# Twenty-four conv and pool pairs and the loop over token chunks: where the side work stands among them

## The reference, cut to what matters

```python
x = layer_norm(x, ln0_g, ln0_b)                  # (2048, 1024)
h = x @ w_in                                     # conv value | conv gate | pool input | queries
a = a_val * sigmoid(a_gate)                      # 384 channels
a = silu(layer_norm(depthwise_conv31(a) + b))
p = trailing_means(p_in, windows 2,4,8,16) - p_in  # 4 groups of 96 channels
p = (p @ pool_w per group) * scale
k, v = mem @ w_mk, mem @ w_mv                    # 256 memory tokens, 4 heads
o = softmax(q @ k.T / 8) @ v
x1 = layer_norm(ALPHA * x + concat(a, p, o) @ w_out)
u = causal_depthwise_conv3(x1 @ w_up)            # 2 x 2816 channels
out = layer_norm(ALPHA * x1 + (silu(u_g) * u_v) @ w_down)
```

## Time and profile before

| what | value |
|---|---|
| median of 3 runs | 2013.52 us (2012.64 to 2013.69) |
| the profiled execution's own time | 2015.45 us |
| its span | 2013.7 us |
| PE busy over the span | 1890.2 us (94%) |
| DVE / ACT / POOL busy | 1483.1 / 940.1 / 259.9 us |
| mean granted clock of PE | 0.976 |

### The profile page before, as it was taken

How to read it: one execution, slowest core, us unless ns; L and a number is a source line. 1 busy time by engine, 2 the same in 40 slices (tenths; PEclk the granted TensorE clock), 3 DMA queues, 4 the chain that set the end, 5 groups by cost and what they waited for, 6 DMA issues and landing times.

```text
span 2013.7 us, 26244 instructions
## 1 busy us (share of the span) xinstructions
PE 1890.2 (94%) x8722; PEld 1572.2 (78%) x8722; DVE 1483.1 (74%) x1892; ACT 940.1 (47%) x1598; POOL 259.9 (13%) x339
## 2 busy tenths in 40 slices
PE   6999998769999899999999899999999897999997
PEld 5788888658788678888888688888887686887786
DVE  5534226558989788888887888778777767566898
ACT  2211124545555465655656665555556334224321
POOL 1101022102212412122120011000000000000111
PEclk9999998979999999999999899999999998999999
DMA  6422234444443834334345333212214557547543
GB/s 219 167 100 84 68 103 145 138 147 146 157 141 136 283 126 146 137 133 143 132 142 188 126 117 134 84 73 94 83 73 162 202 201 281 183 162 262 184 156 126
DMA packets 171788, 296.14 MB, mean 147 GB/s; under 512 B 11713, under 2 KB 106177, under 8 KB 171713
## 3 DMA queue, kind: packets, MB, share of 16 engines
q1 hardware_dynamic: 171712, 295.18, 42.4%
HBM read 189.23 MB, written 105.91 MB: 147 GB/s over the span
## 4 chain that ended last, share of the span: by engine, by line
PE 64%; DVE 11%; DMA 4%; ACT 3%; issue 3%; POOL 0%; SPq 0%; DVEq 0%; ACTq 0%; POOLq 0%
PE banks L2145 54%; PE banks L1090 4%; PE banks L1108 2%; DVE mov_lo L2342 2%; DMA y_scratch<-up_and_out 1%; DMA mov_raw<-wdown_sums_scratch 1%; PE banks L1023 1%; PE banks L1072 1%; DVE sta_lo L2338 1%; DMA mov_raw<-x_operands 1%; ACT mov_hi L2214 1%; PE banks L1054 1%; DVE up_and_out L2376 1%; DVE probs L1542 1%; PE banks L1153 0%
## 5 line engine op out<-in xcount | busy, mean ns | idle before, releaser
L2145 PE MATMUL banks<-mov_hi,sta_hi 128*128 128x512 f32 x1848 | 726.2, 393 | 40.1 <-ACT banks L2221 21.1
L2145 PE MATMUL banks<-mov_lo,sta_hi 128*128 128x512 f32 x1848 | 723.5, 392 | 0.0
L2145 PE MATMUL banks<-mov_hi,sta_lo 128*128 128x512 f32 x1848 | 723.5, 391 | 0.0
L2145 PEld LDWEIGHTS banks<-mov_hi,sta_hi 128*128 128x128 f32 x1848 | 350.2, 190 | 119.4 <-ACT banks L2221 22.7
L2145 PEld LDWEIGHTS banks<-mov_hi,sta_lo 128*128 128x128 f32 x1848 | 349.5, 189 | 73.9
L2145 PEld LDWEIGHTS banks<-mov_lo,sta_hi 128*128 128x128 f32 x1848 | 350.2, 190 | 72.2
L2338 DVE TENSOR_TENSOR sta_lo<-sta_raw,sta_hi 128x512 fp32r<-128x512 f32 (+1 forms) x340 | 224.0, 674 | 62.7 <-ACT sta_hi L2207 60.7
L2207 ACT ACTIVATE sta_hi<-sta_raw 128x512 fp32r<-128x512 f32 (+1 forms) x340 | 198.6, 611 | 135.4 <-PE banks L2145 103.2
L275 PE MATMUL banks<-x0t_hi,win_hi 128*128 128x512 f32 x320 | 126.5, 395 | 1.6 <-DVE x0t_lo L397 1.6
L2236 ACT ACTIVATE half_sums<-banks 128x512 f32<-128x512 f32 x68 | 40.7, 599 | 183.8 <-PE banks L2145 183.8
L275 PE MATMUL banks<-x0t_hi,win_lo 128*128 128x512 f32 x320 | 124.8, 390 | 0.0
(11 more groups left out here) (227 smaller groups left out, 2829.3 us busy)
## 6 DMA issues: line engine op xcount, KB each, us to landing
sta_raw<-in_w_up SPq DMA_DIRECT2D x88, 512.0 KB, 4.1
hidden_scratch<-up_and_out SPq DMA_DIRECT2D x44, 512.0 KB, 2.6
y_scratch<-up_and_out SPq DMA_DIRECT2D x16, 1024.0 KB, 7.5
sta_raw<-hidden_scratch SPq DMA_DIRECT2D x32, 512.0 KB, 4.4
up_and_out<-y_scratch SPq DMA_DIRECT2D x16, 1024.0 KB, 4.9
x_operands<-x_operands_out SPq DMA_DIRECT2D x56, 256.0 KB, 4.1
mov_raw<-x_operands SPq DMA_DIRECT2D x14, 1024.0 KB, 7.3
mov_raw<-in_w_down SPq DMA_DIRECT2D x44, 256.0 KB, 4.6
```

The lines of the kernel that those rows point to most:

```text
L2145: last = pe.matmul(psum, w, x, start=(start and k == 0 and i == 0), stop=(stop and k == m - 1 and i == 2), skip_group_check=True)
```

## The change

- **Start of the pairs.** The last two stores of queries leave the first block's SP list and open the second's; their wait moves to m = 1. PE's wait for the identity moves from before pair 0 to m = 13.
- **Keys, values, fold.** On PE keys go from m = 3 to 4, values from 6 to 7, fold(1) from 11 to 10, scores(0, 1) from 10 to 11; ACT and DVE parts move by a step with them. `bands_out` goes from 5 to 8.
- **Pool pairs in their own places.** Their high and low parts get six buffers of their own (`gp_h`, `gp_l`) instead of those in w_out's last rows; the pool bands move too. So `wout_hi(n >= 3)` waits for the 24 conv groups alone.
- **w_out's last rows** (n = 3 to 7) are loaded and split at m = 15, 16, 18, 20, 21 instead of behind the pairs; conv_total(1, 1) and squares(1, 1), mean(1), deviations(1, 1) come earlier or later as the orders below show. The first two quarters of `project(0)` become `project_first`, which takes the pool rows last.
- **Chunk loop.** `turned_lo(c, 1)` and `turned_hi(c, 1)` come before affine and residual 2 (DVE) and before norm, swish and pooled_hi (ACT); `operand_sums` of all chunks but the last go from POOL to DVE, before `normalise(c, 1)`.

```diff
+            if not is_conv(m):
+                act.wait_ge(prep_lo, 4)
+            act.activation(halves(m)[0][:, :, LEAD:LEAD + QS], gx_raw[:, m % 4, :, :], ACT.Copy).then_inc(gx_hi, 1)
...
-            sp.wait_ge(q_stored, 16 * QT * SEQ // 512)
+            store_last_queries(sp)
...
+                if m in (17, 18, 20):
+                    load_wo({17: 5, 18: 6, 20: 7}[m])
             store_pair(NP - 1)
-            load_wo(5)
-            load_wo(6)
...
-            rstds(0, None)
-            with pool.Fori(1, NCH) as c:
-                rstds(c, c - 1)
-            operand_sums(NCH - 1)
+            with pool.Fori(0, NCH) as c:
+                rstds(c)
+            last_operand_sums()
...
+            def project_first():
+                tok, pooled = slice(0, P), range(CT, 2 * CT)
+                pe.wait_ge(o_lo, 1)
+                pe.wait_ge(c_lo, 1)
+                for ks in ([k for k in range(KT) if k not in pooled], pooled):
+                    if ks is pooled:
+                        pe.wait_ge(p_l, 1)
+                    for b in range(2):
...
-            pe.wait_ge(ident_ok, 3)
             for m in range(NP):
                 pair(m)
-                if m == 3:
+                if m == 4:
                     keys()
-                if m == 6:
+                if m == 7:
                     values()
...
                 if m == 10:
+                    fold(1)
+                if m == 11:
                     scores(0, 1)
-                if m == 11:
-                    fold(1)
                 if m == 13:
+                    pe.wait_ge(ident_ok, 3)
...
                 if m == 21:
+                    turn(1, 1)
                     variance(0)
-                    turn(1, 1)
                 if m == 23:
                     pe.wait_ge(o_lo, 1)
                     attend(1)
+                    pe.wait_ge(c_std, 1)
+                    mean(1)
...
-                    act.wait_ge(g_mm, NG)
+                    act.wait_ge(g_mm, CONV_GROUPS)
...
+                if before2 is not None:
+                    dve.wait_ge(x1t_out, 4 * (before2 + 1))
+                    operand_sums(dve, before2)
                 normalise(c, 1)
...
                 turned_lo(c, 0)
                 scale_conv(c, s)
+                turned_lo(c, 1)
                 if before is not None:
                     affine(before, 0)
                     residual(before, 2)
-                turned_lo(c, 1)
                 conv_lo(c, s)
```

More of the change, by code:

```diff
@@ L139, in columns, with store_queries @@
             return slice(sum(COLS[:part]), sum(COLS[:part + 1]))
+        def store_queries(sp, c):
+            for t in range(QT):
+                row = D_CONV + D_POOL + t * P
+                dst = mix_d[row:row + P, :].rearrange("p (r h q) -> p r h q", r=PHASES, h=2)[:, 4 * (c % 2):4 * (c % 2) + 4, c // 2, :]
+                sp.dma_start(dst, qb[:, t, :].rearrange("p (u q) -> p u q", u=TT)).then_inc(q_stored, 16)
         def turns_behind(c, n):
@@ L678, in groups_done, with halves @@
             return 2 * ORDER.index(n // 2) + n % 2 + 1
+        def halves(m):
+            if is_conv(m):
+                return gx_h[:, m % 3, :, :], gx_l[:, m % 3, :, :]
+            return gp_h[m % 3], gp_l[m % 3]
         def band_place(n):
@@ L714, in store_last_operands, with operand_sums @@
                 sp.dma_start(xop_d[row:row + P, :], src.rearrange("p k t -> p (k t)")).then_inc(done, 16)
+        def operand_sums(eng, c):
+            low_a, up_a, low_b, up_b = xt[:, 0, 0:4, :], xt[:, 0, 4:8, :], xt[:, 1, 0:4, :], xt[:, 1, 4:8, :]
+            if not (isinstance(c, int) and c == 0):
+                eng.wait_ge(xop_stored, 16 * 7 * c)
+            eng.tensor_tensor(xs[:, 0, :, :], up_b, low_b, ALU.subtract).then_inc(x1_sums, 1)
+            eng.tensor_tensor(xs[:, 1, :, :], low_b, low_a, ALU.subtract).then_inc(x1_sums, 1)
+            eng.wait_ge(x1_sums, 4 * c + 2)
+            eng.tensor_tensor(xs[:, 2, :, :], up_b, xs[:, 1, :, :], ALU.subtract).then_inc(x1_sums, 1)
+            eng.wait_ge(x1_sums, 4 * c + 3)
+            eng.tensor_tensor(xs[:, 3, :, :], up_a, xs[:, 2, :, :], ALU.subtract).then_inc(x1_sums, 1)
         def load_x0(sp, c, u):
@@ L982, in _ @@
             last.then_inc(counts_ok, 1)
-            pool.wait_ge(prep_hi, 1)
+            pool.wait_ge(prep_hi, 2)
             for s in used:
@@ L1091, in project @@
                 last.then_inc(y_ready, 1)
+            def project_first():
[6 more added lines that the diff above has]
+                    for b in range(2):
+                        cols = slice(b * 512, (b + 1) * 512)
+                        for k in ks:
+                            for i, (w, x) in enumerate(exact_parts(mx_hi[0][:, k, tok], mx_lo[0][:, k, tok], wo_hi[:, k, cols], wo_lo[:, k, cols])):
+                                last = pe.matmul(ps_y[:, b, :], w, x, start=(k == 0 and i == 0), stop=(k == 2 * CT - 1 and i == 2))
+                        if ks is pooled:
+                            last.then_inc(y_ready, 1)
             def pair(m):
@@ L1098, in pair @@
                     pe.wait_ge(g_out, 2 * m - 4)
[L1099 removed]
+                h, l = halves(m)
                 if is_conv(m):
@@ L1216, in chunk @@
                     turn_x1(before, 0)
-            mean(1)
             pe.wait_ge(wo_l, KT)
-            project(0, 0, 0)
-            project(0, 0, 1)
+            project_first()
             variance(1)
@@ L1396, in _ @@
                     turned_hi(0, 0)
+                if m == 15:
+                    wout_hi(3)
                 if m == 16:
                     turned_hi(0, 1)
+                    wout_hi(4)
                 if m == 17:
@@ L1402, in _ @@
                     attn_hi(0, 0)
+                    wout_hi(5)
                 if m == 19:
@@ L1407, in _ @@
                     turned_hi(1, 0)
+                    wout_hi(6)
+                if m == 21:
+                    wout_hi(7)
                 if m == 22:
@@ L1440, in chunk @@
                 deviation(c)
+                turned_hi(c, 1)
                 if before is not None:
@@ L1444, in chunk @@
                 pooled_hi(c, s)
-                turned_hi(c, 1)
                 attn_hi(c, s)
@@ L1678, in _ @@
                     turned_lo(0, 1)
+                    wout_lo(4)
                 if m == 17:
@@ L1685, in _ @@
                     attn_lo(0, 0)
+                    wout_lo(5)
                 if m == 19:
@@ L1691, in _ @@
                     turned_lo(1, 0)
+                    wout_lo(6)
+                if m == 21:
+                    conv_total(1, 1)
+                    wout_lo(7)
                 if m == 22:
@@ L1694, in _ @@
                     scale_conv(0, 0)
+            dve.wait_ge(g_mm, NG)
             conv_lo(0, 0)
-            wout_lo(3)
-            wout_lo(4)
             attn_lo(1, 1)
-            wout_lo(5)
-            conv_total(1, 1)
-            wout_lo(6)
+            deviations(1, 1)
             pooled_lo(0, 0)
-            wout_lo(7)
             dve.wait_ge(consts, 32)
@@ L1733, in chunk @@
                 attn_lo(c, s)
-            deviations(1, 1)
             residual(0, 0)
@@ L1765, in _ @@
             statistics(NCH - 1, 0)
+            dve.wait_ge(x1t_out, 4 * (NCH - 1))
+            operand_sums(dve, NCH - 2)
             up.lo(first, 1)
```

98 lines of the change are left out of this document (42 added, 56 removed).

## The result

The changed kernel takes 1984.37 us (median of 4 runs, 1982.96 to 1986.11) against 2013.49 (2012.64 to 2013.69) of the kernel before: a ratio of 0.9857, 95% interval 0.9839 to 0.9874, or 29.1 us less. The profiled execution of after took 1982.96 us with a span of 1981.2, that of before 2015.45 with 2013.7, so the two traces lie 32.5 us apart, 3.4 more than the medians. Sums over the traces must be read with that in mind.

A forecast was written before the change was run, and what follows sets the result against it. PE work (94% busy) plus PE's waits was taken to bound the kernel. Pairs 19.5 and loop 7.6 us made 27.1, from 2015.45 to 1988.3 profiled, 1986.5 as median; own range 1981 to 1993, 8 in 10: 1978 to 1998.

The forecast's parts named there:

- Start: Start of the pairs: 1.7 us from a shorter barrier wait, plus 1.4 from matmuls at the upper clock.
- Keys and values: Keys and values one pair later: waits save 4.0 and 2.1 us, clock 4.5 including the start; 12.3 to values' end.
- Fold, ring and transposes: Middle of the pairs: -0.9 wout_lo(2) wait, +4.2 fold_low wait gone, -3.5 pair 15 to turn(1, 1), -0.6 variance(0).
- The walk: Row-by-row estimate of PE's waits from pair 15 to turn(1, 1), which made that stretch 3.5 us longer.
- End of the pairs: Before project: conv_lo alone releases project_first, pooled_lo needed 30 matmuls later; 8.0 us gained, some 5 us wait stays.
- The loop: Chunk loop: turned_lo(c, 1) moved up removes 1.5 us in five chunks, 7.6 us; sums on DVE count 0.
- The third: Rival: the loop gains nothing, DVE with the sums being late elsewhere; 19.5 us alone, 1994 us; chance 0.06.
- The second: Rival: the middle of the pairs gives earlier gains back as waits at the transposes; 17 us left, 1996 us; chance 0.11.
- The first: Rival: the clock also stays up through the pairs and into project; 33 us gained, 1980 us; chance 0.16.
- The fourth: Rival: slower, sums cost DVE 1.5 us each and nothing comes back; chunks of 38.4 us, 2022 us; chance 0.03.
- The fifth: Rival: w_out's loads land late and hold ACT and the pairs; 15 us left, 1998 us; chance 0.04.
- Last chunk: Last chunk: an earlier residual and later sums and loads cancel; 0 us, bounds -2 and +2.

The follow-up runs named there:

- p3_start: The changed kernel with two query stores ahead of the barrier and PE's identity wait at the start of the pairs again: 1988.20 us.
- p2_keys: The changed kernel with keys behind pair 3 and values behind pair 6 again, ACT's and DVE's parts too: 1992.60 us.
- l3_double: The changed kernel with four extra 128x512 subtractions on DVE ahead of operand_sums in each chunk: 1993.26 us.
- p5_fold: The changed kernel with fold(1) and scores(0, 1) in their old order, ACT's and DVE's steps too: 1983.32 us.
- p1_wout_end: The changed kernel with the last five blocks of w_out loaded and split behind the last pair again: 1992.95 us.
- p4_project: The changed kernel with the first two quarters of project in their usual order instead of project_first: 1988.17 us.
- l1_turned: The kernel before, with only turned_hi(c, 1) and turned_lo(c, 1) moved up in the chunk loop, sums still on POOL: 2005.14 us.
- l2_sums: The kernel before, with only the loop's operand sums moved from POOL to DVE, old order kept: 2005.92 us.
- l3_triple: The changed kernel with eight extra 128x512 subtractions on DVE ahead of operand_sums in each chunk: 2017.92 us.

## Why the prediction was right, step by step

The forecast was 27.1 us and 1986.5; measured are 29.1 and 1984.4.

*Start.* Forecast 1.7 us of wait and 1.4 of clock. The wait fell by 1.9, and the first 60 matmuls took 7.41 us instead of 8.93, which is 1.5 of clock. p3_start puts the whole at 3.2 to 3.8. Right.

*Keys and values.* By the end of values and pair 7 the forecast was 12.3; PE was through them at 327.3, before at 340.9, less the 1.1 of the first block: 12.5. p2_keys and p3_start undo it with 8.5 + 3.6 = 12.1 at pair 15, and 8.2 + 3.8 = 12.0 by the medians. Keys kept 1.0 us of wait where 0.7 was forecast. The clock's part was 1.5 at the start, 1.9 in keys (7.88 us, now 6.01) and 1.5 in values (7.50, now 6.02): 4.9, where 4.5 was taken.

*Fold, ring and transposes.* The forecast was -0.9 + 4.2 - 3.5 - 0.6 = -0.8 from there to conv_lo; conv_lo's end moved by 11.6 - 1.1 = 10.5, so it is -2.0. In l3_double, with the same code up to there, it moved 1.2 us more, so the difference from -0.8 is not shown to be more than the spread. fold(0) waited 0.91 for wout_lo(2), as said. But +4.2 and -3.5 were two names for one thing: with fold(1) back at its place (p5_fold) the time is the same, and the wait stands at the first transpose instead of before pair 15. The walk had the waits at their places: 3.2 before pair 15 (forecast 3), 2.6 before turn(0, 1) (4), none, 1.7 and 1.4 at attend(0), scores(1, 1) and turn(1, 0) (1 to 2 each), 6.8 before turn(1, 1) (7). Not foreseen were ACT's waits for the loads of pool pairs, 0.7 and 1.8 us at 364 and 368.

*End of the pairs.* Forecast 8.0; the distance from conv_lo to project fell by 7.9, and p1_wout_end puts the blocks at 8.2 net. The reason, 30 matmuls that cover pooled_lo, holds: without it 3.5 to 4 us are lost (p4_project). Project kept its 5.1 us of wait, as said. By the start of project the pairs gave 18.4 in this trace and 19.7 by that of l3_double (forecast 19.5).

*The loop.* Forecast 7.6, measured 9.7 over the five chunks that had the wait (2 to 6). This is the term that was mis-sized: I took out the wait (1.55) and nothing else, and a chunk fell to 31.85, not 32.3. A wait costs a little more than its row: the pieces of PE overlap at their seams, and the matmuls right behind it run longer (attend takes 3.14 us behind the wait, 3.03 without).

The reason given for this term was half right. The text gave the whole term to the order and 0 to the sums, and said that DVE is covered by 2.4 us. The order alone does carry it (l1_turned, 7.4 us by the medians), and on top of it the sums add little. But l2_sums shows that the sums on DVE take nearly the whole wait away by themselves, which the text did not have: what comes back on DVE is 1.10 for q_lo and about 1 us at each of three sums of the conv statistics, 4.2 us, not 3.1, against 2.8 spent. And l3_double and l3_triple show that the cover was 1.7 us at turned_lo(c, 0), not 2.4 (idle time of DVE) nor 4 (turned_lo(c, 1) before attend). That this did no harm to the forecast is luck: had the 4.2 us not come back, turned_lo(c, 0) would have come 4.2 us later, by these numbers, against 1.7 of cover. Idle time of DVE was not its slack here: the slack is at the first of its results that PE comes for.

*The rivals.* The third, that the loop gains nothing, is out; the trace speaks against the sentence of the Trainium skill's Perfetto Trace Analysis, "Optimizing Scalar/DVE Operations", as I had read it, that offloading between the two engines might not help. That sentence is about relieving a DVE that is full; here the move went the other way, and putting POOL's adds on DVE gave 6.6 us (l2_sums). The second, the middle giving it back, is out by p2_keys. The first, the clock, came in one place of this trace and not for good: project_first's matmuls took 12.5 us, but 13.3 to 14.0 in the other runs behind an equal wait. The fourth stood near a real limit. It was to decide from a DVE cycle of 37 us on, and l3_triple, with chunks of 37.7, is 5.4 us slower than before: the limit fits. But a chunk exceeded DVE's busy time by 3.8 us there (37.7 against 33.9), where the text had put 2.4 on top. Sums of 1.5 us each would have put 3.2 us more on DVE in a chunk, and l3_double lost 1.45 us per chunk with 2.86. With nothing coming back 4.2 more would have been added, 7.4 in all (an estimate from these runs), more than the 5.77 of l3_triple. What excluded the rival was both the 0.69 us, which came in exactly, and the time that came back. The fifth, late loads of w_out, does not show: no wait of PE or ACT among the pairs names a load of w_out.

*Last chunk.* Forecast 0; the 1.7 us of the traces are no more than the spread of p1 to p5, whose code is the same from there on (1355.6 to 1357.7).

Not tested by themselves were the pool pairs' own buffers and the new places of conv_total(1, 1), squares(1, 1), mean(1) and variance(0). What each is worth stays open.

## What to carry to other kernels

When two parts of a change may each cure the same wait, count the wait once and test each part alone: 7.1 and 6.2 us made 7.7 together. Measure the room of an engine not by its idle share but by how early each of its results is before somebody asks for it, and take the smallest (1.7 us here, where the idle time said 3.4). What is gained ahead of a stretch full of waits may be kept all the same: of the 8.5 us of keys and values 8.3 were left behind it. And before a difference of 1 or 2 us between two traces is given a cause, see how far traces of the same code differ at that place.

## What was not expected of the hardware

The time of the matmuls behind one and the same wait is not the same in every run: the first 48 matmuls of project, behind the same 1.85 us of wait on wout_lo and the same 10.3 before it, took 12.51 us in l1_turned and 14.03 in l2_sums, and 14.06 in before. A difference of 1.5 us between two traces at such a place is no finding. The chain rows, l1_turned first:

```profile
428.94 12.51 PE banks L1090 x48
```

```profile
429.03 14.03 PE banks L1090 x48
```

The time that POOL's adds cost DVE reached an instruction that I had not counted: in l1_turned, with POOL adding, four of DVE's operations in a row each take about 1 us longer than in the changed kernel (0.43, 0.68, 0.42 and 0.42 there).

```profile
529.14 1.56 DVE L1553 TENSOR_TENSOR conv_sum<-conv_sum,conv_sq 128x256 f32<-128x256 f32 x1
530.63 1.78 DVE L1514 TENSOR_TENSOR q_lo<-mix_in,q_hi 128x512 fp32r<-128x512 f32 x1
532.33 1.50 DVE L1521 TENSOR_TENSOR conv_sum<-mix_in 128x256 f32<-128x256 f32 x1
533.86 1.40 DVE L1522 TENSOR_TENSOR conv_sum<-conv_sum,mix_in 128x256 f32<-128x256 f32 x1
```
